# Weight slots at 0, 64 and 128 bytes to the operands, and the second operand buffer 128 bytes further on

## The reference

```python
def reference(...):
    # layer 1: h = rmsnorm([meta; x]); zin = h @ w_in            (2048 x 10240, 272 tokens)
    #   q, k, v, gates, pooling input = split(zin)
    #   stick-breaking attention, multiscale pooling, two up-projections,
    #   merged @ w_out, added to x; rmsnorm
    # layer 2: h @ w_in_2 (2048 x 18464): retention and gated delta rule, merged @ w_out_2
    #   cross attention to 256 memory tokens (w_xq, w_xkv, w_xo)
    #   x + square(relu(h @ w_ff1)) @ w_ff2                       (2048 x 8192, 8192 x 2048)
    #   rmsnorm
```

## Time and profile before

| | |
|---|---|
| median of three runs | 2886.94 us (2886.59 to 2888.97) |
| the profiled execution | 2887.99 us, span in the trace 2886.2 us |
| granted TensorE clock | 0.999 of full speed |
| PE matmuls | 15872, busy 2851.5 us (99% of the span) |
| PE weight loads | 15872, busy 2441.1 us |
| VectorE, ScalarE | busy 67% and 47% |
| DMA | 506.66 MB, engines busy 47% |

### The profile page before, as it was taken

One profiled execution on the slowest core, in us unless ns is written; L12 is line 12 of the kernel. 1 busy time (PEld: TensorE's weight loads), 2 busy tenths in 40 slices (PEclk: granted clock), 3 DMA queues, 4 the chain that ended last, 5 costly groups with the idle time before them and its releaser, 6 DMA issues. The chain is left out here.

```text
span 2886.2 us, 38752 instructions
## 1 busy us (share of the span) xinstructions
PE 2851.5 (99%) x15872; PEld 2441.1 (85%) x15872; DVE 1930.9 (67%) x2513; ACT 1354.7 (47%) x1729; POOL 57.1 (2%) x102
## 2 busy tenths in 40 slices
PE   9999999999999999999999999999999999999998
PEld 8899888888888888888888878888888888888887
DVE  7645557678765658888888875466666555656556
ACT  5434644357443445555554543444345433444434
POOL 0000210000000000000000000000000000000000
PEclk9999999999999999999999999999999999999999
DMA  7444445464555544433443345544355445454553
GB/s 279 184 179 161 146 161 195 185 236 171 195 182 196 198 150 159 146 138 140 146 134 139 139 161 203 189 190 146 143 199 188 186 177 202 187 193 179 188 188 146
DMA packets 72849, 506.66 MB, mean 176 GB/s; under 512 B 8384, under 2 KB 8512, under 8 KB 12896
## 3 DMA queue, kind: packets, MB, share of 16 engines
q1 hardware_dynamic: 71136, 497.83, 47.0%
q0 software_dynamic: 1104, 5.90, 0.6%
q10 hardware_dynamic: 432, 0.45, 0.0%
HBM read 499.95 MB, written 2.10 MB: 174 GB/s over the span
## 5 line engine op out<-in xcount | busy, mean ns | idle before, releaser
L1332 PE MATMUL double<-AA,whi 128*128 128x512 f32 (+1 forms) x5008 | 1655.5, 382 | 4.1 <-DVE wlo L2029 3.6
L1332 PE MATMUL double<-AA,wlo 128*128 128x256 f32 (+1 forms) x4624 | 1298.1, 281 | 0.0
L1691 ACT ACTIVATE whi<-raw 128x1024 fp32r<-128x1024 f32 x926 | 925.0, 1049 | 794.3 <-PE double L1332 761.5
L2029 DVE TENSOR_TENSOR wlo<-raw,whi 128x1024 fp32r<-128x1024 f32 (+1 forms) x934 | 1101.0, 1213 | 235.0 <-ACT whi L1691 232.4
L1332 PEld LDWEIGHTS double<-AA,whi 128*128 128x128 f32 x5008 | 915.2, 188 | 196.9 <-DVE wlo L2029 5.1
L1332 PEld LDWEIGHTS double<-AA,wlo 128*128 128x128 f32 x4624 | 870.0, 188 | 1.5
L1332 PE MATMUL double<-whi,AA 128*128 128x512 f32 x1536 | 487.8, 393 | 0.5 <-DVE wlo L2029 0.5
L1332 PEld LDWEIGHTS double<-whi,AA 128*128 128x128 f32 x1536 | 288.5, 188 | 60.8 <-DVE wlo L2029 1.3
L1332 PE MATMUL double<-whi,BB 128*128 128x512 f32 x1024 | 322.3, 394 | 0.0
L1332 PE MATMUL double<-wlo,AA 128*128 128x512 f32 x768 | 299.1, 389 | 0.0
L1332 PEld LDWEIGHTS double<-whi,BB 128*128 128x128 f32 x1024 | 192.9, 188 | 45.0
(11 more groups left out here) (335 smaller groups left out, 1721.5 us busy)
## 6 DMA issues: line engine op xcount, KB each, us to landing
raw<-in_wall SPq DMA_DIRECT2D x462, 1024.0 KB, 4.9
raw<-in_wall SPq DMA_DIRECT2D x9, 256.0 KB, 6.4
X<-in_xT SPq DMA_DIRECT2D x1, 2048.0 KB, 11.3
Mm<-in_memT POOLq DMA_DIRECT2D x1, 2048.0 KB, 15.9
tmp<-rqk POOLq DMA_DIRECT2D x16, 128.0 KB, 2.2
mblk<-in_memT SPq DMA_DIRECT2D x8, 256.0 KB, 5.0
dec<-in_dec POOLq DMA_DIRECT2D x1, 1536.0 KB, 9.1
hs<-in_hsT SPq DMA_DIRECT2D x4, 272.0 KB, 5.4
```

The costliest lines, as they stand in the source:

```text
L1332: return q.matmul(out, lhsT, rhs, start=start, stop=stop, skip_group_check=True)
L1691: q.activation(whi[j % SPL][:, c], raw[j % RAW][:, c], ACT.Copy).then_inc(S("w_hi"), 1)
L2029: return q.tensor_tensor(out, a, b, o)
```

## The change

The two list comprehensions that place the slots become a loop that moves the arena ahead before each slot, so that slot i lies at 64 x i bytes to the first buffer by 256. `whi` and `wlo` of a slot now follow each other (before, the three `whi` came first). After the slots, the arena is moved so that AA lies at 0 again, and before BB it is moved so that BB lies at AA's place by 256: from 128 to 0. What is allocated behind BB moves with it. No instruction, semaphore or order changes.

```diff
     ar = Arena(base)
     raw = [ar.get([P_, UNIT], F32, f"raw{i}") for i in range(RAW)]
-    whi = [ar.get([P_, UNIT], F32R, f"whi{i}") for i in range(SPL)]
-    wlo = [ar.get([P_, UNIT], F32R, f"wlo{i}") for i in range(SPL)]
+    whi, wlo = [], []
+    w0 = ar.off
+    for i in range(SPL):
+        ar.off += (w0 + 64 * i - ar.off) % 256
+        whi.append(ar.get([P_, UNIT], F32R, f"whi{i}"))
+        wlo.append(ar.get([P_, UNIT], F32R, f"wlo{i}"))
+    ar.off += (w0 - ar.off) % 256
     A_off = ar.off
     AA = ar.get([P_, 2, NT * L], F32R, "AA")
...
+    ar.off += (A_off - ar.off) % 256
     boff = ar.off
     BB = ar.get([P_, 2, 8 * T], F32R, "BB")
```

## The result

| | before | after |
|---|---|---|
| median, 13 runs each | 2888.07 us | 2892.50 us |
| range | 2886.59 to 2890.37 | 2891.37 to 2894.58 |
| ratio (95% interval) | | 1.0016 (1.0009 to 1.0023) |
| the profiled execution | 2887.99 us, span 2886.2 | 2894.06 us, span 2892.3 |

So the changed kernel is 4.4 us slower by the medians, clear of noise by the interval, but inside the 0.2% that the prediction had called no change. The forecast was 2889 (range 2870 to 2902). In the traces the difference is 6.1 us.

A forecast was written before the change was run, and what follows sets the result against it. PE's matmul steps were taken to set the end. Terms 4.4 + 2.2 - 2.9 - 1.4 + 0.3 + 0 - 0.2 = +2.4 us on the profiled 2887.99 gave 2890.4, a median of 2889, range 2870 to 2902.

The forecast's parts named there:

- What bounds the kernel: PE's steps from matmul to matmul set the end; PE busy 2851.5 of 2886.2 us, producers of weights have time to spare.
- point 7: ScalarE's and VectorE's slot writes at 64 and 128: even a tenth more lies in ScalarE's 761.5 us of waiting; cost 0.
- points 1 and 2: 512-column matmuls with weights moving: with AA +4.4 us (slot 2) and +2.2 (slot 1); with BB -2.9 and -1.4.
- points 3 and 6: Weights-stationary pairs, AA at a constant place: new distance each 16-pair unit mixes both beats, 350.4 ns a pair, +0.3 us.
- point 6: Entering a unit: every 16 pairs start at a new distance, so no beat carries over 60 us; a mixture is likelier.
- points 4 and 5: Matmuls whose operand goes round four places: 0; weights-stationary pairs with BB, from 351 to 350.4 ns, -0.2 us.
- the slower one: Rival: slots 1 and 2 leave the good distance, steps 232.3 ns and 353.1 a pair; +12 us, about 2899; chance 0.25.
- All short: Rival: a fresh distance every 16 pairs keeps PE out of the long beat; -9.5 us, about 2877; chance 0.22.
- Addresses do nothing: Rival: the two operand buffers differ for another reason, such as their stages; time 2887; chance 0.08.

## Why the prediction was right, and where it was not

- What bounds the kernel: right. PE's steps alone moved; its wait for `wlo` went from 4.2 to 3.4 us. The cover of the writers (point 7) was not even needed, their means stayed at 1050 and 1220 ns.
- Kind N (points 1 and 2): right in mechanism and in size. Slot 2 at 232.8 ns (forecast 232.3), slot 1 at 229.6, where 229.5 was the middle taken between two rows; +5.0 us with AA for a forecast of +6.6, and -3.6 for -4.3 in f2. The middle was luck for 64: at 96 or 192 the same choice would have been 4 ns off, as the table shows.
- Kind T at a constant place (points 3 and 6): the step that failed. The forecast took a mixture of both beats, 350.4 ns a pair and +0.3 us, and point 6 argued that short stays at one distance make a mixture likely. In the changed kernel each slot instead keeps one beat from stage to stage: 353.1, 353.2 and 350.3 in slots 0, 1 and 2. So 64 has no short beat, and 0, which had it in xo and in four blocks of f1 before, is long behind 128 in every undisturbed stretch (two units behind a pause, in mk and xq, took 347.6). The stages cost +4.3 us. The mean over these units, 352.3, would be +6.5 us on the forecast's count of 3328 pairs. The undisturbed stages (wo, wo2, xo, f1) took +3.5 of it; those with side work between the matmuls took only 0.8, with nearly half the pairs.
- The going-round kinds and kind T with BB (points 4 and 5): right, -0.5 and +0.3 us.
- The rivals: the slower one named this place, and half of it came: the long beat in slots 0 and 1, but kind N at 64 dearer by only half. "All short" had the right idea, that a distance can force the short beat, and the wrong distances. "Addresses do nothing" is refuted by the run with BB alone. The Trainium skill's "SBUF — State Buffer", "Who interferes with whom", gives TensorE two independent read ports. If that were all, the distance of the two operands would cost nothing; the traces do not agree, 226.7 ns at 0 against 232.8 at 128.
- The range was honest about the two beats; the point was 3.5 us low.

Open: why a distance has the beat it has. Open too: what picks the beat where a distance has two. That the stream of the moving operand and the weight load for the next matmul meet in memory is the reading I hold, since only their distance counts, but no run here shows the meeting itself: each was seen only as a step.

## What to carry to other kernels

Where PE sets the end with back-to-back fp32r matmuls, measure the step (stretch over count), one stage and one buffer at a time (a row's mean is not the cost, though over one stage alone it did move with the step: 389 ns in mv and 395 in f2, before): a steady loss with no wait behind it may be the distance of the two operands. Try the distances by 256 in steps of 32 bytes, several in one run by giving each slot its own, and choose one for each kind of matmul; here 0 for moving weights, and 96 for stationary ones in four stages (wo2, xq, xo, f1), were worth 0.5%, 0.2% of which came with BB's move alone. Don't scatter the slots: a place that is bad for one kind spoils a third of it, and what runs before a stage can change its beat.

## What the runs showed of the hardware that I had not expected

- The step of a 512-column fp32r matmul hangs on where its operands lie to each other: 226.7 ns at 0, 229.6 at 64, 233 at 32, 96, 192 and 224, 234 at 160; with everything 64 bytes further on, the times were the same to 0.01 us a unit.
- The sign counts: weights 64 above the operand 229.6 ns, 64 below it 233.1.
- One program place can have two steady beats: wo, with the same addresses, took 353.1 ns a pair in the kernel before and 346.7 with BB alone moved, each kept for all of its 89 to 90 us. Distances 32 and 192 have two as well (346.9 and 353.1, 348.9 and 353.5).
- DMA traffic of 0 or 301 GB/s beside a unit left its step unchanged (5.55 us each).
